# Moving the conditioning matmuls of groups 3 to 11 out of layer 0's feed-forward

## The chip, the cores and the metric

The kernel runs on one core of a Trainium2 chip. The time is that of one execution on the device, in microseconds (us); of the kernel before, three executions took 1819.61, 1820.89 and 1824.89 us, with a median of 1820.89 us.

## What is computed

Two transformer blocks of two layers each run one after the other on 256 latent tokens and 256 context tokens of width 1024. Layers 0 and 1 are the first block, layers 2 and 3 the second. The reference, cut to what matters here (`rms` is the RMS norm, `c` the conditioning vector):

```
shift1, scale1, gate1, shift2, scale2, gate2 = split(silu(c) @ w_ada[i] + b_ada[i], 6)
h = rms(x, g1) * (1 + scale1) + shift1             # norm n1
x = x + gate1 * (mixer(h) @ w_out[i])              # attention and others; layer 3: pooling
h = rms(x, g2) * (1 + scale2) + shift2             # norm n2
x = x + gate2 * (conv_ffn(h) @ w_down[i])          # w_up, 3-tap convolution, silu(gate) * value
# layers 2 and 3: the mixer's and the feed-forward's outputs pass a further RMS norm (p1, p2) before the gate
```

The six modulation vectors of a layer come from a matrix of 1024 x 6144 applied to two conditioning vectors (latent and context). They depend on no token: any time before their first use will do.

## The kernel before, in words

Activations lie transposed, with the 1024 channels as 8 tiles of 128 partitions and the tokens along the free axis: 512 tokens in layer 0, 256 from layer 1's mixer output on. Every weight block (128 output columns, 512 KB; 320 or 384 KB in w_down) is loaded by SyncE into one of four buffers `RAW`, split by ScalarE into a high part `WHI` (hi_split) and by VectorE into a remainder `WLO` (lo_split), and used by TensorE in `products`, which issues three matmuls for each of the block's k tiles: high x high, high x low and low x high. A block of w_up is 24 matmuls. A layer has the stages norm n1, projection (`proj`), attention, `w_out` (8 blocks), in layers 2 and 3 norm p1, then norm n2, `w_up` (44 blocks), `w_down` (32 blocks), and in layers 2 and 3 norm p2. Each engine has its own instruction queue, written out by hand in program order, and runs it in order; semaphores join them.

The conditioning matrices are cut into 12 groups of 8 units, three groups to a layer (3l, 3l + 1, 3l + 2). Group 0 is done at the start. A unit is 1 MB of weights, loaded by a DMA that GpSimd (POOL) issues, and four matmuls with 512 columns of weights moving (`mod_kt`, L1446; the trace shows each as two, so 8 per unit), all of a group adding up in PSUM bank 4. When 8 units are done, ScalarE copies the bank to `ROW` (`row_out`), TensorE transposes it (`mod_turn`, L1463), and VectorE adds the result to `MOD` (`mod_apply`). `derive` makes the norm's factors from `MOD`.

Before the change, groups 1 and 2 stand in layer 0's projection and use two buffers in turn, `GWA` and `GWB`. Group 3 stands in layer 0's w_out, one unit behind each block, and groups 4 to 8 and half of 9 in layer 0's w_up, one unit behind each of the 44 blocks; all these use the one buffer `GWA`, so that POOL issues the next load only when TensorE has used the unit before (L478, waiting for `gw_used`). The rest of 9, and 10 and 11, stand in layer 0's w_down with four buffers `GWH`. From layer 1 on TensorE runs no conditioning work.

A norm goes like this: squares (ScalarE), their sums by TensorE (`acc_sum`, L1470, where VectorE has added the squares up along the way; or `norm_sums`, L1478, 32 matmuls with one column), the root on ScalarE (L603), the reciprocal on VectorE (L950), its spread over the partitions by TensorE (L1493), and then VectorE (L1009, L999) and ScalarE (L616) write the 8 tiles of the next stage's input one by one.

## Time and profile before

| | us |
|---|---|
| three executions, median | 1820.89 |
| the profiled execution | 1823.76 |
| its span, first to last instruction | 1822.1 |
| TensorE busy (92% of the span) | 1671.3 |
| VectorE busy | 995.3 |
| ScalarE busy | 808.1 |
| POOL busy | 112.9 |

The profile is of one execution. "PE" is TensorE's matmuls and "PEld" its weight loads; an engine's idle time is put down to what ended it. TensorE's granted clock is 1.00 (2.4 GHz) or 0.50 (1.2 GHz) in each stretch; over the span its mean is 0.956. Its slices over the span (40 equal ones, tenths) and those of the DMA rate are

```profile
PEclk9999999899999999998999999989989999679999
GB/s 377 208 187 171 1 1 139 128 219 214 234 211 233 206 257 250 276 105 104 127 24 47 149 180 172 174 144 113 24 93 151 184 159 181 75 94 183 184 160 118
```

### The profile page before, as it was taken

What the parts mean: (1) busy time and instruction counts of PE and PEld (TensorE: products, weight loads), DVE (VectorE), ACT (ScalarE), POOL (GpSimd) and SP (SyncE); (2) the same over time, 40 slices, a digit from 0 to 9 for tenths busy, and PEclk for the clock granted to TensorE, in tenths of its full rate; (3) what the DMA queues carried; (4) which work ended last, traced back from release to release, by engine and by line L of the source; (5) the groups of instructions that cost most, each with busy time, mean ns of one, the idle gap of its engine ahead of it and who ended that gap; (6) DMA issues with size and microseconds to landing.
All of it is one profiled execution on the core that took longest, in us unless ns stands there. A gap on an engine that the chain in (4) does not pass through costs nothing.

```text
span 1822.1 us, 30331 instructions
## 1 busy us (share of the span) xinstructions
PE 1671.3 (92%) x10760; PEld 1395.0 (77%) x10760; DVE 995.3 (55%) x1746; ACT 808.1 (44%) x1406; POOL 112.9 (6%) x150
## 2 busy tenths in 40 slices
PE   3999998789999999998999999989889999589997
PEld 1786686566666666677958899979679999479997
DVE  3434863544444442226475888565556664666654
ACT  3314662333333322124364666443545555445543
POOL 0240000000000010001300000002000000000000
PEclk9999999899999999998999999989989999679999
DMA  9654003366666577733401455643035656236654
GB/s 377 208 187 171 1 1 139 128 219 214 234 211 233 206 257 250 276 105 104 127 24 47 149 180 172 174 144 113 24 93 151 184 159 181 75 94 183 184 160 118
DMA packets 72369, 285.06 MB, mean 156 GB/s; under 512 B 8001, under 2 KB 11329, under 8 KB 60513
## 3 DMA queue, kind: packets, MB, share of 16 engines
q1 hardware_dynamic: 58528, 187.31, 32.7%
q0 software_dynamic: 13760, 96.67, 15.2%
q8 instruction: 52, 0.85, 0.2%
q14 instruction: 29, 0.23, 0.0%
HBM read 282.90 MB, written 1.05 MB: 156 GB/s over the span
## 4 chain that ended last, share of the span: by engine, by line
PE 72%; DMA 14%; DVE 8%; issue 3%; ACT 2%; POOL 1%; SPq 0%; POOLq 0%; DVEq 0%; ACTq 0%
PE B L1425 17%; PE B L1427 17%; PE B L1426 17%; DMA GWA<-in_wmod 12%; PE B L1446 5%; PE B L1586 3%; PE B L1616 3%; DVE NORM L1009 2%; PE B L1604 1%; PE B L1478 1%; DMA MW<-in_wmod 1%; DVE HL L999 1%; PE B L1438 1%; PE B L1440 1%; PE B L1439 1%
## 5 line engine op out<-in xcount | busy, mean ns | idle before, releaser
L1425 PE MATMUL B<-HH,WHI 128*128 128x256 f32 (+1 forms) x1872 | 614.4, 328 | 46.6 <-DVE HL L999 24.8
L1426 PE MATMUL B<-HL,WHI 128*128 128x256 f32 (+1 forms) x1872 | 597.0, 319 | 0.0
L1427 PE MATMUL B<-HH,WLO 128*128 128x256 f32 (+1 forms) x1872 | 596.9, 319 | 0.0
L919 DVE TENSOR_TENSOR WLO<-RAW,WHI 128x1024 fp32r<-128x1024 f32 (+1 forms) x376 | 414.7, 1107 | 249.0 <-ACT WHI L559 248.1
L559 ACT ACTIVATE WHI<-RAW 128x1024 fp32r<-128x1024 f32 (+1 forms) x376 | 358.9, 959 | 256.6 <-PE B L1427 254.5
L1425 PEld LDWEIGHTS B<-HH,WHI 128*128 128x128 f32 x1872 | 363.8, 194 | 128.7 <-issue 84.3
L1427 PEld LDWEIGHTS B<-HH,WLO 128*128 128x128 f32 x1872 | 364.4, 195 | 23.3
L1426 PEld LDWEIGHTS B<-HL,WHI 128*128 128x128 f32 x1872 | 365.4, 195 | 19.0
L1425 PE MATMUL B<-MIDH,WHI 128*128 128x256 f32 (+1 forms) x704 | 220.5, 313 | 0.0
L1427 PE MATMUL B<-MIDH,WLO 128*128 128x256 f32 (+1 forms) x704 | 218.1, 310 | 0.0
L1426 PE MATMUL B<-MIDL,WHI 128*128 128x256 f32 (+1 forms) x704 | 218.0, 310 | 0.0
L1266 DVE SCALAR_TENSOR_TENSOR Y<-B,VEC,Y 128x255 f32<-128x255 f32 (+1 forms) x132 | 75.4, 571 | 220.1 <-ACT Y L805 114.7
L1425 PEld LDWEIGHTS B<-MIDH,WHI 128*128 128x128 f32 x704 | 134.4, 191 | 23.7 <-issue 17.6
L1427 PEld LDWEIGHTS B<-MIDH,WLO 128*128 128x128 f32 x704 | 134.4, 191 | 7.3
L1426 PEld LDWEIGHTS B<-MIDL,WHI 128*128 128x128 f32 x704 | 134.5, 191 | 6.2
L805 ACT ACTIVATE Y<-B,VEC 128x256 f32<-128x256 f32 (+1 forms) x88 | 54.3, 617 | 136.0 <-PE B L1427 133.6
L1586 PE MATMUL B<-KP,QK 128*128 128x512 f32 (+1 forms) x192 | 89.6, 564 | 8.7 <-ACT PB L719 7.6
L1069 DVE TENSOR_REDUCE SM<-B 128x1 f32<-128x512 f32 (+1 forms) x112 | 68.4, 611 | 42.6 <-PE B L1586 21.2
L1269 DVE SCALAR_TENSOR_TENSOR Y<-B,VEC,Y 128x255 f32<-128x255 f32 (+1 forms) x132 | 75.5, 572 | 17.9 <-DVE Y L1266 2.1
L1446 PE MATMUL B<-GWA,CV 128*32 128x512 f32 x480 | 63.9, 604 | 20.9 <-DMA GWA<-in_wmod 20.4
L719 ACT ACTIVATE PB<-B,SM 128x512 f32<-128x512 f32 (+1 forms) x112 | 69.7, 625 | 25.9 <-DVE SM L1075 15.2
L732 ACT ACTIVATE PTS<-B 128x512 f32<-128x512 f32 (+1 forms) x88 | 47.3, 538 | 54.4 <-PE B L1604 53.8
(172 smaller groups left out, 1652.7 us busy)
## 6 DMA issues: line engine op xcount, KB each, us to landing
RAW<-in_wup SPq DMA_DIRECT2D x176, 512.0 KB, 3.8
GWA<-in_wmod POOLq DMA_DIRECT2D x60, 1024.0 KB, 5.3
RAW<-in_wdn SPq DMA_DIRECT2D x64, 384.0 KB, 3.2
RAW<-in_wproj SPq DMA_DIRECT2D x44, 512.0 KB, 3.9
RAW<-in_wdn SPq DMA_DIRECT2D x64, 320.0 KB, 3.3
GWH<-in_wmod POOLq DMA_DIRECT2D x20, 1024.0 KB, 6.0
RAW<-in_wout SPq DMA_DIRECT2D x24, 512.0 KB, 3.6
MW<-in_wmod SPq DMA_DIRECT2D x4, 2048.0 KB, 18.5
```

The lines of the kernel that those rows point to most:

```text
L559: act_f(WH[s][:, 0:kts, :], RAW[s][:, 0:kts, :], ACT.Copy).then_inc(hi_done, 1)
L719: act_f(PB[:, u % 4, 0:nk], SBANK[u % 3][:, 0:nk], ACT.Exp, bias=SM[:, 320 + u:321 + u], scale=SCALE[it["kind"]], accum_out=SM[:, 384 + u: ...
L919: v.tensor_tensor(WL[s][:, 0:kts, :], RAW[s][:, 0:kts, :], WH[s][:, 0:kts, :].bitcast(F32), ALU.subtract).then_inc(lo_done, 1)
L1069: link(v.tensor_reduce(SM[:, 256 + u:257 + u], SBANK[u % 3][:, 0:nk], AX.X, ALU.max))
L1266: v.scalar_tensor_tensor(out=y[:, :, 1:256], in0=b[:, :, 0:255], scalar=w(0, which), in1=y[:, :, 1:256], op0=ALU.mult, op1=ALU.add).then_i ...
L1269: v.scalar_tensor_tensor(out=y[:, :, 0:255], in0=b[:, :, 1:256], scalar=w(2, which), in1=y[:, :, 0:255], op0=ALU.mult, op1=ALU.add).then_i ...
L1425: mm(bank[:, 0:t], wh, a, start=first and k == 0, stop=False)
L1426: mm(bank[:, 0:t], wh, b, start=False, stop=False)
L1427: ins = mm(bank[:, 0:t], wl, a, start=False, stop=stop and k == kts - 1)
L1446: ins = mm(GB[32 * j:32 * j + 32, :], CV[:, 4 * kt:4 * kt + 32], W[:, j, :], start=kt == 0, stop=kt == 7)
L1586: ins = mm(bank[:, 0:b - a], store[:, q, P * qt:P * qt + P], keys[:, k, a:b], start=True, stop=not window)
L1616: ins = mm(OBANK[it["grp"] % 2][:, c:c + it["dv"]], PTS[:, i % 2, P * k:P * k + P], it["val"](it["keys"][0] // P + k), start=k == 0, stop= ...
```

## The change

The 72 units of groups 3 to 11 are placed anew. In TensorE's order they now stand at these places:

- layer 0: two units inside w_out; two between w_out's last block and the sums of norm n2; one between the sums and the spread of n2, three behind the spread (group 3). None in w_up or w_down before the last block.
- behind the last block of w_down in layers 0, 1 and 2: two units each, then one before and two (in layer 2: five) behind the spread of the norm that follows (groups 4, 7, 10).
- layer 1: 11 units in the projection's slots 2 to 12 (rest of group 4, and group 5), 8 units behind the last 8 blocks of w_up (group 6).
- layer 2: 3 units in the projection (rest of 7), two behind w_out, one before and five behind the spread of p1 (group 8), 8 behind the last 8 blocks of w_up (group 9).
- layer 3: four units behind the spread of n1 and four behind that of p1 (group 11).

The transposes (`mod_turn`) of groups 3, 6 and 9 stand in the first block of the next w_down, those of 4, 5 and 7 in the projections, those of 8, 10 and 11 between the sums of the norms n2 of layer 2, n1 of layer 3 and n2 of layer 3. There the copy to `ROW` stands on ScalarE between the third and the fourth pair of squares, and `mod_apply` and `derive` on VectorE ahead of the reciprocal.

Each unit has a home buffer (`HOMES`): `A` and `B` as before, `H0` to `H3` in the input tiles `HH` and `HL`, `R0` to `R10` and `K0`, `K1` in the space of the attention's and feed-forward's intermediates. POOL waits before a load for the last unit with the same home, and, where the space is that of something else, for the block after which it is free. So seven loads are now issued one behind the other once w_out's first block is done in layer 0, five at the start of w_down in layer 0, four at w_out in layer 1, seven at the start of w_down in layer 1, five in w_out and eight or nine at the start of w_down in layer 2. ScalarE waits in two norms (`H_UNITS`) until the units in `H0` to `H3` are used. The total of units, matmuls and bytes is unchanged. `mod_apply` waits for its own add in the new code.

```diff
+HOMES = {1: "A B A B A B A B", 2: "A B A B A B A B", 3: "A R0 R1 R2 R3 R4 R5 R6", 4: "H0 H1 H2 H3 A B A B",
+         5: "A B A B A B A B", 6: "A R6 R8 R9 R10 A R6 R8", 7: "H0 H1 H2 H3 R6 A R8 A",
+         8: "A K0 K1 R5 R6 R8 R9 R10", 9: "A R6 R8 R9 R10 A R6 R8", 10: "H0 H1 H2 H3 R6 A R8 R9",
+         11: "R10 R6 A R8 R9 R10 R6 A"}
...
+PROJ_UNITS = [{i: (1 + i // 8, i % 8) for i in range(16)},
+              {i + 2: ((4, 5 + i) if i < 3 else (5, i - 3)) for i in range(11)},
+              {2: (7, 5), 4: (7, 6), 7: (7, 7)}]
...
-        GWB = sb("GWB", [P, 4, 512], at=w0 + 69632)
-        GWH = [sb(f"GWH{s}", [P, 4, 512], at=hhat + 8192 * s) for s in range(4)]
+        GW = {"A": GWA, "B": sb("GWB", [P, 4, 512], at=w0 + 69632)}
+        for s in range(4):
+            GW[f"H{s}"] = sb(f"GWH{s}", [P, 4, 512], at=hhat + 8192 * s)
+        for s in (0, 1, 2, 3, 4, 5, 6, 8, 9, 10):
+            GW[f"R{s}"] = sb(f"GWR{s}", [P, 4, 512], at=w0 + 8192 * s)
+        for s in range(2):
+            GW[f"K{s}"] = sb(f"GWK{s}", [P, 4, 512], at=w0 + 20480 + 8192 * s)
...
+        H_UNITS = {(1, "n1"): 28, (2, "n1"): 52}
+        TURNED = {(2, "n2"): 8, (3, "n1"): 10, (3, "n2"): 11}
...
-            def unit(u, used, W, ready):
+            def unit(g, kt):
+                u = 8 * (g - 1) + kt
+                if unit_before(u) is not None:
+                    gp.wait_ge(gw_used, unit_before(u) + 1)
+                gp.dma_start(GW[HOME[u]][:].rearrange("p a b -> p (a b)"), A["wmod1"][u * P:u * P + P, :]
+                             ).then_inc(gw_ready[HOME[u]], 16)
...
-                    if l == 0 and i < 14:
-                        unit(i + 2, i + 1, GWB if i % 2 else GWA, gwb_ready if i % 2 else gwa_ready)
+                    if l == 2 and i == 3:
+                        unit(7, 7)
+                    if l < 2 and i + 2 in PROJ_UNITS[l] and (l == 0 or i >= 1):
+                        unit(*PROJ_UNITS[l][i + 2])
...
-            with gp.Fori(16, 68, 1) as u:
-                unit(u, u, GWA, gwa_ready)
+            unit(3, 0)
+            gp.wait_ge(blk_used, OUT0[0] + 1)
+            for kt in range(1, 8):
+                unit(3, kt)
             gp.wait_ge(blk_used, DOWN0[0])
-            for s in range(4):
-                unit(68 + s, 0, GWH[s], gwh_ready[s])
-            with gp.Fori(1, 5, 1) as i:
-                for s in range(4):
-                    unit(68 + 4 * i + s, 65 + 4 * i + s, GWH[s], gwh_ready[s])
-            for l in (1, 2):
-                tables(l)
-                proj(l)
+            for kt in range(5):
+                unit(4, kt)
+            tables(1)
+            unit(4, 5)
+            proj(1)
+            gp.wait_ge(nl_ready, 8 * ROUND[1, "n1"] + 8)
+            gp.dma_start(X[:, :, 256:512], A["ctx2"].rearrange("p (k t) -> p k t", k=KT)).then_inc(ctx2_in, 16)
+            unit(6, 0)
+            gp.wait_ge(blk_used, OUT0[1] + 1)
+            for kt in range(1, 8):
+                unit(6, kt)
+            gp.wait_ge(blk_used, DOWN0[1])
+            for kt in range(7):
+                unit(7, kt)
+            tables(2)
+            proj(2)
+            for kt in range(3):
+                unit(8, kt)
+            gp.wait_ge(blk_used, OUT0[2] + 1)
+            for kt in range(3, 8):
+                unit(8, kt)
+            for kt in range(8):
+                unit(9, kt)
+            gp.wait_ge(blk_used, DOWN0[2])
+            for kt in range(8):
+                unit(10, kt)
+            unit(11, 0)
             tables(3)
+            for kt in range(1, 8):
+                unit(11, kt)
...
+                if key in H_UNITS:
+                    act.wait_ge(gw_used, H_UNITS[key])
...
+                        if c == 2 and key in TURNED:
+                            row_out(TURNED[key])
...
+                if key in TURNED:
+                    mod_apply(TURNED[key], 1)
+                    for slot in {(2, "n2"): (1, 3), (3, "n1"): (2,), (3, "n2"): (1, 3)}[key]:
+                        derive(l, slot)
...
+                        if kt == 6 and key in TURNED:
+                            mod_turn(TURNED[key])
                         norm_sum(r, kt, kt // 2 % 2, 256, kt == 0, 256 * (kt % 2))
+                if key in FILL_ROOT:
+                    fill(*FILL_ROOT[key])
                 pe.wait_ge(rr_ready, r + 1)
                 for q in range(nt):
                     ins = nc.tensor.transpose(RB[:, P * q:P * q + P], RR[:, q:q + 1].broadcast_to((P, P)), ident)
                 ins.then_inc(rb_ready, 1)
+                if key in FILL_SPREAD:
+                    fill(*FILL_SPREAD[key])
+            FILL_ROOT = {(0, "n2"): (3, [4]), (1, "n1"): (4, [2]), (2, "n1"): (7, [2]), (2, "p1"): (8, [2]),
+                         (2, "p2"): (10, [2])}
+            FILL_SPREAD = {(0, "n2"): (3, [5, 6, 7]), (1, "n1"): (4, [3, 4]), (2, "n1"): (7, [3, 4]),
+                           (2, "p1"): (8, [3, 4, 5, 6, 7]), (2, "p2"): (10, [3, 4, 5, 6, 7]),
+                           (3, "n1"): (11, [0, 1, 2, 3]), (3, "p1"): (11, [4, 5, 6, 7])}
...
-                    if l == 0:
-                        mod_unit(3, m, GWA, gwa_ready, 128 + 16 * (m + 1))
+                    if l == 0 and m in (2, 5):
+                        fill(3, [m // 3])
+                if l != 1:
+                    fill(3 if l == 0 else 8, [2, 3] if l == 0 else [0, 1])
                 acc_sum(r, t)
...
-                        if l == 0:
-                            kt = kt0 + s
-                            if kt == 0:
-                                mod_turn(group - 1)
-                            mod_unit(group, kt, GWA, gwa_ready, 128 * group - 256 + 16 * (kt + 1))
+                        if kt0 is not None:
+                            mod_unit(6 if l == 1 else 9, kt0 + s)
...
+                    with pe.Fori(0, FT // 2 - 2, 1) as i:
+                        body(i, False)
+                    body(FT // 2 - 2, False, kt0=0)
+                    body(FT // 2 - 1, True, kt0=4)
...
-                            if l == 0:
-                                b = 4 * a + s
...
+                            if l < 3 and isinstance(i, int) and i == 0 and a == 0 and s == 2:
+                                mod_turn((3, 6, 9)[l])
...
+                if l < 3:
+                    fill((4, 7, 10)[l], [0, 1])
                 acc_sum(r, tn)
```

In TensorE's queue, these rows stand in layer 0's w_up loop before: the last matmuls of a block, the transposes of the group before, the unit, and the next block.

```order
L1426 MATMUL B<-HL,WHI 128x512
L1427 MATMUL B<-HH,WLO 128x512
L1459 REGISTER_ALU
L1461 REGISTER_ALU
L1463 MATMUL B<-CST,ROW 128x128 x4
L1452 ISA
L1446 MATMUL B<-GWA,CV 32x512 x4
L1683 REGISTER_ALU
L1684 REGISTER_ALU
L1425 MATMUL B<-HH,WHI 128x512
```

And these now, where one block of that loop ends and the next begins:

```order
L1467 MATMUL B<-HL,WHI 128x512
L1468 MATMUL B<-HH,WLO 128x512
L1746 REGISTER_ALU
L1747 REGISTER_ALU
L1466 MATMUL B<-HH,WHI 128x512
```

The unit and the transposes have left; block follows block.

In TensorE's queue, between the last block of layer 2's w_out and the first of its w_up, that is around the norms p1 and n2, before:

```order
L1427 MATMUL B<-HH,WLO 128x256
L1470 MATMUL B<-CST,ACC 128x1 x2
L1493 MATMUL B<-CST,RR 128x128 x2
L1478 MATMUL B<-CST,SQ 128x1 x16
L1493 MATMUL B<-CST,RR 128x128 x2
```

and now:

```order
L1487 MATMUL B<-GWA,CV 32x512 x4
L1487 MATMUL B<-GWK_96,CV 32x512 x4
L1518 MATMUL B<-CST,ACC 128x1 x2
L1487 MATMUL B<-GWK_97,CV 32x512 x4
L1545 MATMUL B<-CST,RR 128x128 x2
L1487 MATMUL B<-GWR_91,CV 32x512 x4
L1487 MATMUL B<-GWR_92,CV 32x512 x4
L1487 MATMUL B<-GWR_93,CV 32x512 x4
L1487 MATMUL B<-GWR_94,CV 32x512 x4
L1487 MATMUL B<-GWR_95,CV 32x512 x4
L1526 MATMUL B<-CST,SQ 128x1 x12
L1511 MATMUL B<-CST,ROW 128x128 x4
```

All eight units of group 8 now stand ahead of the second norm's sums, and its transposes inside them.

In POOL's queue, in layer 1's projection, before (`RE<-SM` is one projection's roots copied out for the spread, `KP<-QK` the padded keys):

```order
L508 COPY RE<-SM 128x256
L518 TENSOR_SCALAR KP<-QK,CST 128x512 x2
L508 COPY RE<-SM 128x256
L518 TENSOR_SCALAR KP<-QK,CST 128x512 x4
L508 COPY RE<-SM 128x256
```

and now, where each load waits until TensorE has used the unit two slots back:

```order
L510 DMA GWB<-in_wmod 128x2048
L537 COPY RE<-SM 128x256
L547 TENSOR_SCALAR KP<-QK,CST 128x512 x2
L510 DMA GWA<-in_wmod 128x2048
L537 COPY RE<-SM 128x256
L547 TENSOR_SCALAR KP<-QK,CST 128x512 x4
L510 DMA GWB<-in_wmod 128x2048
```

A load stands ahead of each slot's copies, and behind the key copies of the slot before.

## Rows read from the trace of the kernel before

**Rows 1.** The page's chain that ended last, shares of the span by engine and line.
```profile
PE B L1425 17%; PE B L1427 17%; PE B L1426 17%; DMA GWA<-in_wmod 12%; PE B L1446 5%; PE B L1586 3%; PE B L1616 3%; DVE NORM L1009 2%; PE B L1604 1%; PE B L1478 1%; DMA MW<-in_wmod 1%; DVE HL L999 1%; PE B L1438 1%; PE B L1440 1%; PE B L1439 1%
```

**Rows 2.** The chain in order of time, a load in layer 0's w_up: start, duration.
```profile
409.61 5.44 DMA GWA<-in_wmod
```

**Rows 3.** TensorE's waits: layer 0's w_out, then 344.3 to 671.3: total, times, longest.
```profile
PE B L1446 <- DMA GWA<-in_wmod: 5.0, 7, 1.4
...
PE B L1446 <- DMA GWA<-in_wmod: 15.4, 33, 3.2
```

**Rows 4.** Timeline of TensorE, w_up and w_down of layer 0: start, duration.
```profile
416.67 0.39 PE L1427 MATMUL B<-HH,WLO 128*128 128x512 f32 x1
...
421.67 0.60 PE L1463 MATMUL B<-CST,ROW 128*128 128x128 f32 x4
422.19 1.07 PE L1446 MATMUL B<-GWA,CV 128*32 128x512 f32 x8
...
684.28 0.39 PE L1427 MATMUL B<-MIDH,WLO 128*128 128x512 f32 x1
684.60 1.06 PE L1446 MATMUL B<-GWH,CV 128*32 128x512 f32 x8
685.59 0.50 PE L1425 MATMUL B<-MIDH,WHI 128*128 128x512 f32 x1
685.93 0.39 PE L1426 MATMUL B<-MIDL,WHI 128*128 128x512 f32 x1
```

**Rows 5.** Windows: us, PE, PEld, DVE, ACT, POOL busy (x), PEclk, DMA share, GB/s.
```profile
350.50:671.30 320.80, 303.85 (x1432) 206.51 (x1432) 152.02 (x204) 112.10 (x151) 23.64 (x45) 0.99 0.60 211
...
1143.00:1157.00 14.00, 14.00 (x119) 14.00 (x118) 7.93 (x12) 6.65 (x10) 0.00 (x0) 1.00 0.64 183
1364.90:1494.00 129.10, 129.09 (x1056) 128.81 (x1057) 89.74 (x141) 74.42 (x116) 0.00 (x0) 0.98 0.55 163
```

**Rows 6.** Timeline of TensorE around the norms of layers 0 and 1.
```profile
344.38 1.05 PE L1470 MATMUL B<-CST,ACC 128*128 128x1 f32 x8 [1.12 <-DVE ACC L1228]
...
350.53 0.76 PE L1425 MATMUL B<-HH,WHI 128*128 128x512 f32 x1 [3.42 <-DVE HL L999]
...
358.31 0.50 PE L1425 MATMUL B<-HH,WHI 128*128 128x512 f32 x1 [0.61 <-DVE HL L999]
...
819.87 1.87 PE L1470 MATMUL B<-CST,ACC 128*128 128x1 f32 x8 [2.44 <-DVE ACC L1228]
```

**Rows 7.** Timeline of TensorE, norms p1 and n2 of layer 2, p1 and n2 of layer 3.
```profile
1350.55 0.60 PE L1470 MATMUL B<-CST,ACC 128*128 128x1 f32 x4 [0.93 <-DVE ACC L1228]
1351.71 0.43 PE L1493 MATMUL B<-CST,RR 128*128 128x128 f32 x2 [0.55 <-DVE RR L950]
1354.84 6.99 PE L1478 MATMUL B<-CST,SQ 128*128 128x1 f32 x32 [2.70 <-ACT SQ L594]
...
1599.00 4.93 PE L1478 MATMUL B<-CST,SQ 128*128 128x1 f32 x32 [1.73 <-ACT SQ L594]
...
1608.25 6.99 PE L1478 MATMUL B<-CST,SQ 128*128 128x1 f32 x32 [3.07 <-ACT SQ L594]
```

**Rows 8.** The chain at the kernel's start: 16 matmuls, two units back to back.
```profile
33.23 1.97 PE B L1446 x16
```

**Rows 9.** Windows in the stretches behind norms, columns as in rows 5.
```profile
345.50:355.50 10.00, 6.09 (x14) 3.55 (x15) 8.53 (x23) 5.46 (x13) 0.00 (x0) 0.50 0.26 100
1352.50:1369.00 16.50, 11.76 (x50) 11.02 (x51) 13.07 (x26) 7.60 (x15) 0.00 (x0) 0.50 0.21 65
```

**Rows 10.** DMA queues, 678:685, w_down of layer 0: packets, MB, share (q0 POOL's, q1 SyncE's).
```profile
q0 software_dynamic: 315, 2.31, 78.4%
q1 hardware_dynamic: 268, 0.68, 24.5%
```

**Rows 11.** Timeline of POOL, layer 1's projection, and TensorE's one wait for it.
```profile
873.40 6.74 POOL L518 TENSOR_SCALAR KP<-QK,CST 128x512 f32<-128x512 f32 x4
...
880.54 0.44 PE L1521 MATMUL B<-CST,RE 128*128 128x128 f32 x2 [1.67 <-POOL RE L508]
```

More of the change, by code:

```diff
@@ L786, in w_out, with body @@
                         tile_squares(l, "out", m, m % 2, bank)
-                    if l == 0 and m == 7:
-                        row_out(3)
             def w_up(l):
                 t = TT[l]
-                def body(i, last, group=None):
+                def body(i, last):
                     for j in range(2):
@@ L823, in body @@
                             mid_hi, 1)
-                    if group is not None:
-                        row_out(group)
                 def split(n4, s, last):
@@ L862, in body @@
                                 tile_squares(l, "down", 2 * i + a, a, banks[a])
-                            if l == 0 and a == 1 and s == 3 and not last:
-                                row_out(9 + i)
+                            if l in (1, 2) and isinstance(i, int) and i == 0 and a == 0 and s == 0:
+                                row_out(6 if l == 1 else 9)
                 loop(act, KT // 2, body, peel=True)
@@ L898, in _ @@
                 norm((l, "n2"))
+                if l == 0:
+                    row_out(3)
                 w_up(l)
@@ L1195, in attention @@
                         v_squares()
[L1196 to L1200 removed]
+                    if j == 6:
+                        if l < 2:
+                            mod_apply((2, 5)[l], 0)
+                        derive(l, 1 if l < 2 else 2)
                     if IS_L[l] and j == TT[l] // 32 + 5:
@@ L1247, in seg, with body @@
                     return ap.rearrange("p (s t) -> p s t", s=ns)
-                def body(i, last, group=None, second=0):
+                def body(i, last):
                     for j in range(2):
@@ L1292, in body @@
                                             ALU.subtract).then_inc(mid_lo, 1)
-                        if group is not None and j == 0:
-                            mod_apply(group, second)
-                if l:
-                    loop(dve, FT // 2, body)
-                else:
-                    for second, (a, b) in enumerate(((0, 3), (3, 5))):
-                        with dve.Fori(a, b, 1) as d:
-                            body(2 * d, False, group=3 + d, second=second)
-                            body(2 * d + 1, False)
-                    body(FT // 2 - 1, True, group=8, second=1)
+                loop(dve, FT // 2, body)
             def w_down(l):
@@ L1390, in _ @@
                 if l:
-                    for slot in range(2 if IS_L[l] else 4):
-                        derive(l, slot)
+                    derive(l, 0)
                 norm((l, "n1"))
```

95 lines of the change are left out of this document (37 added, 58 removed).

## The prediction

> **What bounds the kernel now.** I read the page's chain of waits first: its three largest entries are the products, 17% each, and the fourth is a DMA, the load into `GWA`, with 12% [rows 1]. Next the chain in order of time, to see what that load does in layer 0's w_up: when a unit ends, its successor's load takes 5.44 us [rows 2], and then the next unit runs 1.1 us [rows 4]. So there a block lasts as long as the single buffer's cycle. TensorE isn't idle in it, since its 24 matmuls lie beside the load; it waits only 5.0 us in w_out and 15.4 us up to the end of w_up [rows 3]. The chain's 12% is therefore no measure of the gain: nearly all of it is also matmul time. Then the timeline, for the price of the products and of a unit [rows 4], and the windows, for the stages and for who else is busy [rows 5]. TensorE sets the pace in every w_up and w_down; VectorE is busy 152 of 321 us in layer 0's w_up and 90 of 129 in layer 2's [rows 5].
>
> **Prices.** In w_up of layer 0 the start of one matmul lies 0.227 us behind the other (5.00 us for 22, to the transposes), so a block of 24 is 5.45 us [rows 4]. A unit between two blocks: from the last matmul of one to the second of the next pass 1.65 us [rows 4]; two intervals of 0.227 would pass anyway, so a unit costs 1.19 us. Two units in a row take 1.97 us [rows 8]. The transposes take 0.52 us [rows 4].
>
> **What leaves layer 0.** In w_out six of eight units go. Eight at 1.19 and 5.0 us of waits are 14.5; two come back, 2.4, and the wait for the summed squares, 1.12 us when the last unit covered part of it, becomes the 2.44 us that it is where none stands before it [rows 6], 1.3 more. Left: 10.8 us. In w_up all units go. The 44 blocks need 44 x 5.45 = 239.8 us, and the first one 4.7 more, since it goes tile by tile behind VectorE: it begins at 350.53, its sixth tile at 358.31, and with the last nine matmuls it ends near 360.7 [rows 6]. That is 244.5 against 320.8 [rows 5], so 76.3 us less. In w_down, from 671.3, where w_up ends, to the sums at 819.87 are 148.6 us [rows 5, 6]; 528 matmuls at 0.227, one set of transposes and the 2.44 us wait make 122.9. That is 25.7 less. Sum for layer 0: 112.8 us. It needs no other engine to be faster: at 245 us VectorE's 152 us are 62%, below what it carries in layer 2's w_up (70%) where TensorE doesn't wait [rows 5].
>
> **What comes to the later layers.** Thirty units stand among matmuls that set the pace: 11 and 3 in projections, 8 and 8 at the ends of two w_ups. At 1.19 us they cost 35.7 us. Four sets of transposes (groups 4, 6, 7, 9) add 2.1; those of group 5 stand before attention, where TensorE waits anyway, and I take them as nothing (0.5 if not). The `row_out` copies, `mod_apply` and `derive` go to ScalarE and VectorE while they have slack, and in the three turned norms they lie beside the sums; at nothing, 0.6 us in each if the cover is too short.
>
> Forty units stand at norms. Layer 0's n2 and the n1 of layers 1 and 2: two units behind the last block fill the 2.4 us wait. One before the spread stands in a gap of about 0.55 us [rows 7], so the spread comes 0.4 late in layers 0 and 1; those behind it fit into 3.42 us [rows 6]. ScalarE's new wait ends one unit behind the spread, when VectorE's first tile is just written. In layer 1 the sums take 1.87 us at the low clock against 1.05 in layer 0 [rows 6]; with no idle time before them I expect 1.05. Together 0.4 + 0.4 - 0.8 = 0.0 us.
>
> The p1 of layer 2 is tighter. Two units (1.97) against a wait of 0.93: 1.0 late. One against 0.55: 0.4 late. Five behind the spread, 4.9 us, against 2.70: 2.2 late. Transposes inside the sums: 0.5. Against this the 32 one-column matmuls last 6.99 us at clock 0.50, and 4.93 where they began at full clock [rows 7, 9]; I take 4.93, a gain of 2.1. Sum +2.0 us. The p2 of layer 2 with layer 3's n1 has the same pattern, +2.0. Layer 3's p1 with n2: four units, 3.9, against 3.07, transposes 0.5, the same gain of 2.1: -0.7 [rows 7]. Norms in all: +3.3 us. From both sides: if those sums all ran at full clock (about 3.5 us each), 4 us less; if the units and sums there ran at the low clock, some 17 us more, because a unit then takes about 1.8 times as long, by the ratio of the sums' 1.87 to 1.05 [rows 6].
>
> **The loads.** Before, at most four units were in flight while weights were wanted slowly. Where both queues were full, POOL's got 2.31 MB in 7 us, 330 GB/s, and the weights' 0.68 MB, 97 GB/s [rows 10]. A w_down of 256 tokens wants 183 GB/s [rows 5]. Layer 1's w_down now begins with seven loads: 7.3 MB at 330 GB/s, 22 us, in which the weights miss 86 GB/s x 22 = 1.9 MB. Four `RAW` buffers of about 0.36 MB are ahead, 1.4 MB; the 0.5 MB left take 2.6 us at 183 GB/s. Layer 2's begins with nine: 28.6 us, 2.5 MB missed, 1.0 MB not covered, 5.6 us. Bounds: nothing, if more is ahead than four buffers (four more are already split), and twice as much, if the clock falls in the waits. I take 8.2 us. The bursts in w_out (four and five loads) miss less than the four full blocks ahead; nothing. In layer 0's w_out the weights are wanted at half the rate; nothing.
>
> In layer 1's projection POOL is the narrow place: one slot's copies of the keys take 6.74 us, and TensorE once waited 1.67 us for it [rows 11]. The new loads stand between those copies, each for a unit two slots later. Two loads go out right behind such a copy, and I count 1.5 us of waits above the one that was there; between 2 less (slots longer by a unit let POOL catch up) and 8 more.
>
> **Sum.** -112.8 + 35.7 + 2.1 + 3.3 + 8.2 + 1.5 = -62.0 us. The profiled execution took 1823.76 us, so its like takes 1761.8. It is 2.9 above the median of the three; from the median 1820.89 the forecast is 1759 us.
>
> **A rule weighed.** Behind layer 0's n2 the granted clock is 0.50 for 10 us, but TensorE is busy 6.09 of them and still waits for VectorE's tiles once the clock is back [rows 6, 9]. So I give nothing for a clock that stays high there. The Trainium skill ("TensorE: Matmul & The Clock Gate", Terms) puts the penalty of throttled time at that time multiplied by one minus the granted ratio, which would be 5 us here.
>
> **Rivals.**
>
> First, more than that. The weights keep up in both w_downs (8.2 back), POOL catches up (2), the sums run at full clock (4): 14 less, 1745 us. For it: eight blocks, not four, are prepared ahead at full tilt. Against: the weights get only 97 of 183 GB/s for over 20 us. Chance 0.23.
>
> Second, the clock pays. The units keep TensorE busy behind three norms (layer 0's n2, n1 of layers 1 and 2), the clock stays at 1.00, and half of three stretches of 10 us comes back: 15 less, 1744 us. Against: VectorE's pace there, 1.57 us for a tile where three matmuls at the low clock need 1.4. Chance 0.05. This is what the skill's rule for throttled time would give.
>
> Third, the norms at the low clock and the squeeze doubled: 17 + 8 more, 1784 us. For it: sums of one column went along with a clock of 0.50 in 1352.5 to 1369 [rows 9], so that the units behind them may find it low. Against: the units are dense work just ahead. Chance 0.13.
>
> Fourth, the change doesn't do what it says in layer 0: w_up keeps a slower pace though the units are gone, because the conversion chain (ScalarE, then VectorE, for each block) was hidden by the 7 us cycle. At 6.2 instead of 5.45 us for 44 blocks, 33 more, 1792 us. Against: layer 2's w_up has a chain of the same length with blocks of 2.94 us (129.1 / 44), and TensorE is busy all the time [rows 5]. Chance 0.03.
>
> Fifth, slower than before: the late units miss their loads. Each of the 30 then waits in TensorE's queue with all later matmuls behind it. At the longest wait seen, 3.2 us [rows 3], that is 96 us: 1759 - 1.5 + 96 = 1853. It turns the sign from 2.1 us of wait for each unit (62 / 30). Against: two buffers in turn, and at the w_ups' ends five of eight units loaded long before. Chance 0.02. The skill ("DMA: Bandwidth & Descriptors", SWDGE vs HWDGE vs iDMA) says that VectorE can lock GpSimd out of the memory in which it writes its descriptors, which would delay just these loads; no row here shows it.
>
> **Chances and range.** The forecast has 0.54, with 1750 to 1768 as its own range; the rivals have 0.23, 0.05, 0.13, 0.03 and 0.02. For a range that holds 8 in 10 I go down to 1744 and up to 1778. About 0.3% is what a measurement of this kernel can tell from no change: faster 0.97, same 0.01, slower 0.02.
>
> **What would show it.** Right: no `GWA` wait in layer 0's w_up, and that stage 244 to 246 us; w_down of layer 0 about 122 us; units beside the norms at 1.0 us each and the sums of layer 2's n2 near 5 us; w_down of layer 1 and of layer 2 about 3 and 6 us longer than their 528 matmuls take at the pace of that layer's w_up (2.94 us for 24, so 64.6 us), with TensorE waiting for `WLO` and POOL's queue full beside it. Wrong: TensorE waiting for `WLO` or `drained` banks in layer 0's w_up; units of layer 1's projection waiting over 2 us each; half-clock stretches behind layer 2's p1 longer than the 16.5 us there were [rows 9]; a w_down of layer 1 with no wait at all.

## The result and the profile after

The changed kernel takes 1757.84 us (median of four executions, 1755.87 to 1759.65), the kernel before, measured beside it, 1820.25 (1817.82 to 1824.89): a ratio of 0.9654, with a 95% interval of 0.9632 to 0.9676. The forecast was 1759. The profiled execution of after took 1755.87 us with a span of 1753.7, that of before 1823.76 and 1822.1.

The page of the changed kernel: spans by engine, the clock's slices, and the two rows of the chain that answer to [rows 1]; `products` now stands in L1466 to L1468, a unit in L1487.

```profile
PE 1643.3 (94%) x10760; PEld 1389.6 (79%) x10760; DVE 995.4 (57%) x1746; ACT 808.1 (46%) x1406; POOL 112.6 (6%) x150
...
PEclk8999999999999999999989999999999999889999
...
PE 84%; DVE 9%; DMA 4%; ACT 2%; issue 1%; POOL 0%; SPq 0%; DVEq 0%; ACTq 0%
PE B L1466 22%; PE B L1468 21%; PE B L1467 21%; PE B L1487 4%; PE B L1646 3%; PE B L1676 3%; DMA RAW<-in_wdn 2%; DVE NORM L1064 2%; PE B L1664 2%; DMA MW<-in_wmod 1%; DVE SM L1124 1%; PE B L1479 1%; PE B L1481 1%; PE B L1480 1%; DVE HL L1054 1%
```

The load into `GWA` is gone from the chain, and the products went from 17% to 21 or 22% each. What is new in it is the DMA `RAW<-in_wdn`, 2%: SyncE's weights for w_down.

Windows of after (us, PE, PEld, DVE, ACT, POOL busy, PEclk, DMA share, GB/s): layer 0's w_up, the 10 us around its start, then the w_downs of layers 1 and 2.

```profile
341.08:585.18 244.10, 241.10 (x1056) 197.74 (x1057) 151.05 (x197) 109.09 (x145) 0.00 (x0) 1.00 0.31 91
...
336.00:346.00 10.00, 7.52 (x47) 2.98 (x48) 8.47 (x23) 5.49 (x13) 0.00 (x0) 1.00 0.01 2
...
1050.00:1120.00 70.00, 67.04 (x556) 64.51 (x548) 37.09 (x51) 32.07 (x44) 4.06 (x8) 1.00 0.82 280
1419.00:1492.00 73.00, 68.99 (x557) 66.06 (x549) 29.94 (x41) 31.02 (x51) 5.04 (x10) 0.98 0.82 286
```

Layer 0's w_up takes 244.10 us where it took 320.80 [rows 5], with the same VectorE work (151 us); VectorE's share rose from 47% to 62%.

The stages, each from the start of one marking instruction to that of the next (a stage's first product, or the first sum of a norm), in the traces of before and after:

| stage | before | after | difference | forecast |
|---|---|---|---|---|
| w_out, layer 0 | 62.6 | 50.6 | -12.0 | -10.8 |
| w_up, layer 0 | 320.8 | 244.1 | -76.7 | -76.3 |
| w_down, layer 0 | 148.6 | 122.7 | -25.8 | -25.7 |
| all norms, from their first sum on, with layer 3's pooling | 97.4 | 93.2 | -4.2 | +1.3 |
| layer 1, projection to w_out | 182.1 | 194.4 | +12.3 | +15.1 |
| w_up, layers 1 and 2 | 258.6 | 276.8 | +18.2 | +19.0 |
| w_down, layers 1 and 2 | 130.1 | 142.4 | +12.4 | +10.2 |
| layer 2, projection to w_out | 136.5 | 141.0 | +4.5 | +5.1 |
| all before layer 0's w_out, all of layer 3 behind its n2 | 485.5 | 488.4 | +2.9 | 0 |
| sum | 1822.1 | 1753.7 | -68.4 | -62.0 |

(The forecast's transposes and late sums are counted here in the stage in which they stand.) The spans differ by 6 us more than forecast, the medians by 62.4 as forecast: the profiled execution of before lay 3.5 us above its median, that of after 2.0 below.

TensorE's timeline around layer 0's n2, start and duration, which answers to [rows 6]:

```profile
332.55 1.92 PE L1487 MATMUL B<-GWR,CV 128*32 128x512 f32 x16
335.04 1.05 PE L1518 MATMUL B<-CST,ACC 128*128 128x1 f32 x8 [0.56 <-DVE ACC L1282]
336.02 1.06 PE L1487 MATMUL B<-GWR,CV 128*32 128x512 f32 x8
337.02 0.65 PE L1545 MATMUL B<-CST,RR 128*128 128x128 f32 x4
337.60 2.78 PE L1487 MATMUL B<-GWR,CV 128*32 128x512 f32 x24
341.08 0.47 PE L1466 MATMUL B<-HH,WHI 128*128 128x512 f32 x1 [0.70 <-DVE HL L1054]
...
345.72 0.50 PE L1466 MATMUL B<-HH,WHI 128*128 128x512 f32 x1 [0.61 <-DVE HL L1054]
...
348.88 0.50 PE L1466 MATMUL B<-HH,WHI 128*128 128x512 f32 x1 [0.61 <-DVE HL L1054]
```

Six units fill the waits: the one for the summed squares, 1.12 us before behind one unit and 2.44 where no unit stood before it [rows 6], is 0.56, and 3.42 became 0.70. In the kernel before, the clock was 0.50 from 5 us ahead of w_up's first product to 5 us behind it [rows 9]; the same stretch of after, 336 to 346 above, has 1.00. And yet the tiles begin at the same pace: the sixth 7.80 us behind the first (341.08, 348.88), before 7.78 (350.53, 358.31 [rows 6]). In that kernel's trace the second and the fourth tile, 3.15 us apart at half clock, were

```profile
352.01 0.79 PE L1425 MATMUL B<-HH,WHI 128*128 128x512 f32 x1
...
355.16 0.67 PE L1425 MATMUL B<-HH,WHI 128*128 128x512 f32 x1
```

and in the changed kernel's two intervals at full clock are 3.16 us (345.72 to 348.88). TensorE waits about 0.6 us for VectorE's `HL` before each of these tiles now: VectorE sets the pace. What gained from the clock is the spread, which waits for no tile: 0.65 us above, and 1.11 in the kernel before:

```profile
346.00 1.11 PE L1493 MATMUL B<-CST,RR 128*128 128x128 f32 x4 [0.57 <-DVE RR L950]
```

The same around layer 2's p1 and n2, which answers to [rows 7]:

```profile
1268.04 1.06 PE L1487 MATMUL B<-GWK,CV 128*32 128x512 f32 x8
1269.04 0.43 PE L1545 MATMUL B<-CST,RR 128*128 128x128 f32 x2
1269.40 4.50 PE L1487 MATMUL B<-GWR,CV 128*32 128x512 f32 x40
1273.83 2.91 PE L1526 MATMUL B<-CST,SQ 128*128 128x1 f32 x24
1276.60 0.63 PE L1511 MATMUL B<-CST,ROW 128*128 128x128 f32 x4
1277.07 0.95 PE L1526 MATMUL B<-CST,SQ 128*128 128x1 f32 x8
```

The 32 one-column matmuls took 6.99 us at half clock; they take 2.91 + 0.95 = 3.86 now. The sums begin late, because of five units, and end early all the same.

### The profile page after: what moved, and what is told of

The parts are those of the page before. It is cut to its first block, busy times and chain, and to the rows that moved or that the text cites. A ratio compares the mean times of both kernels' runs of the same rounds, so it can differ in the third digit from the quotient of the medians.

```text
span 1753.7 us, 29978 instructions
## 1 busy us (share of the span) xinstructions
PE 1643.3 (94%) x10760; PEld 1389.6 (79%) x10760; DVE 995.4 (57%) x1746; ACT 808.1 (46%) x1406; POOL 112.6 (6%) x150
## 4 chain that ended last, share of the span: by engine, by line
PE 84%; DVE 9%; DMA 4%; ACT 2%; issue 1%; POOL 0%; SPq 0%; DVEq 0%; ACTq 0%
PE B L1466 22%; PE B L1468 21%; PE B L1467 21%; PE B L1487 4%; PE B L1646 3%; PE B L1676 3%; DMA RAW<-in_wdn 2%; DVE NORM L1064 2%; PE B L1664 2%; DMA MW<-in_wmod 1%; DVE SM L1124 1%; PE B L1479 1%; PE B L1481 1%; PE B L1480 1%; DVE HL L1054 1%
## 5 line engine op out<-in xcount | busy, mean ns | idle before, releaser
L1466 PE MATMUL B<-HH,WHI 128*128 128x256 f32 (+1 forms) x1872 | 607.4, 324 | 36.4 <-DVE HL L1054 21.2
L1468 PE MATMUL B<-HH,WLO 128*128 128x256 f32 (+1 forms) x1872 | 594.2, 317 | 0.0
L1466 PEld LDWEIGHTS B<-HH,WHI 128*128 128x128 f32 x1872 | 362.5, 194 | 94.3 <-issue 45.8
L1468 PEld LDWEIGHTS B<-HH,WLO 128*128 128x128 f32 x1872 | 363.1, 194 | 22.2
L1466 PE MATMUL B<-MIDH,WHI 128*128 128x256 f32 (+1 forms) x704 | 220.0, 313 | 7.0 <-DVE WLO L969 6.9
L1468 PE MATMUL B<-MIDH,WLO 128*128 128x256 f32 (+1 forms) x704 | 218.5, 310 | 0.0
L1466 PEld LDWEIGHTS B<-MIDH,WHI 128*128 128x128 f32 x704 | 135.0, 192 | 17.0 <-DVE WLO L969 8.4
L1468 PEld LDWEIGHTS B<-MIDH,WLO 128*128 128x128 f32 x704 | 135.0, 192 | 6.8
L1124 DVE TENSOR_REDUCE SM<-B 128x1 f32<-128x512 f32 (+1 forms) x112 | 68.4, 611 | 41.4 <-PE B L1651 20.8
L878 ACT ACTIVATE MIDH<-Y 128x256 f32 (+3 forms) x88 | 40.8, 463 | 57.5 <-DVE Y L1333 57.5
```

What stands on the lines that cost most here:

```text
L1124: link(v.tensor_reduce(SM[:, 256 + u:257 + u], SBANK[u % 3][:, 0:nk], AX.X, ALU.max))
L1466: mm(bank[:, 0:t], wh, a, start=first and k == 0, stop=False)
L1468: ins = mm(bank[:, 0:t], wl, a, start=False, stop=stop and k == kts - 1)
```

## The experiments

Each ran beside the kernel before on the same chip, in three sets. The median of the kernel before was 1819.1 us in the first (spaced loads, half the bytes, no unit in slot 8), 1818.93 in the second (the changed kernel once more, earlier loads, idle places, the three together) and 1819.73 in the third (short units, the second version). Ratios are to it, with their 95% intervals. In the diffs, + is the experiment and ... stands for parts left out.

**The changed kernel once more**, as the control.

> The changed kernel once more, for the comparison on this chip: 1756 to 1759, ratio to the kernel before 0.965.

1755.62 us, ratio 0.9656 (0.9635 to 0.9677), span 1754.0. Every stage lies within 0.5 us of the first trace, but for layer 0 up to n2 (3 us shorter) and layer 1's projection to w_out (3.0 us longer; its wait for `GWB` was 3.2 us).

**Loads spaced.** The bursts of seven and nine loads in the w_downs of layers 1 and 2 become one load per four and three blocks.

```diff
-            gp.wait_ge(blk_used, DOWN0[1])
             for kt in range(7):
+                gp.wait_ge(blk_used, DOWN0[1] + 4 * kt)
                 unit(7, kt)
...
```

> The changed kernel, with the loads of groups 7, 10 and 11 at the start of layer 1's and layer 2's w_down not issued one behind the other but one for every 4 blocks (layer 1) or 3 blocks (layer 2). Theory: the waits of 3.0 and 4.0 us for WLO in these two stages, the slower blocks beside them and the low clock behind them come from POOL's loads taking the DMA engines from the weights. Then both stages lose their waits, w_down of layer 1 gets some 4 us shorter and that of layer 2 some 6 us, and the time falls from 1757.8 to about 1748. Rival: the waits come from the transposes in the first block or from the order of the conversions; then they stay, and the time with them (1757 to 1759).

1749.7 us, ratio 0.9627 (0.9609 to 0.9646). Queues in 1051 to 1063, w_down of layer 1, first of the changed kernel, then of the spaced one (packets, MB, share; q1 is SyncE's, q0 POOL's):

```profile
q0 software_dynamic: 530, 3.95, 83.9%
q1 hardware_dynamic: 292, 0.73, 15.3%
```

```profile
q1 hardware_dynamic: 576, 1.44, 39.0%
q0 software_dynamic: 222, 1.69, 37.9%
```

And TensorE's wait in that w_down, in the changed kernel (the spaced one has none for `WLO`):

```profile
PE B L1466 <- DVE WLO L969: 3.0, 3, 1.6
```

With a burst in flight the weights get 0.73 MB in these 12 us, 61 GB/s; without it 1.44 MB, and TensorE doesn't wait for them. The burst does it in two ways. SyncE issued a load at 1052.63, and no packet of it moved before 1056.0; in the spaced kernel one issued at 1052.60 had moved 148 packets by then. After that both queues are busy and share by packets, not by bytes. From 1057 to 1072 in the changed kernel:

```profile
q0 software_dynamic: 643, 4.65, 74.2%
q1 hardware_dynamic: 639, 1.60, 27.3%
```

The stage went from 69.97 to 66.09 us, that of layer 2 from 72.47 to 66.00: the squeeze cost 3.9 + 6.5 = 10.4 us. The stages repeat well: layer 1's w_down took 69.9 to 70.1 us in all six traces that have the whole burst and 66.1 in the four in which it is spaced or halved. By medians the spaced kernel is only 5.9 us below the control, and 8.1 below the first measurement; its profiled execution was its fastest, 3.8 us below its median, so the size rests on the stages. Of the 10.4 us TensorE's waits for `WLO` are 3.0 + 4.0 = 7.0. Another 1.5 is a stretch at half clock in layer 2, right behind the last of these waits, where 16 matmuls start 0.216 us apart instead of 0.120:

```profile
1449.00:1452.40 3.40, 3.40 (x19) 3.40 (x18) 0.82 (x1) 0.79 (x2) 0.00 (x0) 0.51 0.93 364
```

The remaining 1.9 weren't traced. Without the squeeze the two stages take 66 us against 65.6 and 64.5 before; 0.5 of that are the transposes.

**Half the bytes, after.** Each unit of groups 3 to 11 loads 0.5 MB and multiplies it twice.

```diff
-                gp.dma_start(GW[HOME[u]][:].rearrange("p a b -> p (a b)"), A["wmod1"][u * P:u * P + P, :]
+                gp.dma_start(GW[HOME[u]][:, 0:(2 if g > 2 else 4), :].rearrange("p a b -> p (a b)"),
+                             A["wmod1"][u * P:u * P + P, 0:(1024 if g > 2 else 2048)]
...
```

> The changed kernel, but each unit of groups 3 to 11 loads only half of its weights (0.5 MB) and its four matmuls use that half twice; matmuls and waits are as many as before. Theory: what loads cost in the changed kernel is the squeeze in the two w_downs (some 10 us) and the wait in layer 1's projection (up to 4 us): 1744 to 1748. Rival: the loads cost nothing and the waits have another reason: 1757 to 1759. A second rival: the loads also slow the matmuls or conversions elsewhere, then well below 1740.

1741.52 us, ratio 0.9583 (0.9561 to 0.9606). The w_downs take 66.09 and 65.83 us, the same as with spaced loads, by another way; layer 1's projection to w_out 191.06 instead of 194.43, with one wait of 1.4 us for `GWB`. So the bytes cost about 14 us in the changed kernel: 10.5 in the two w_downs and 3.4 there.

**Half the bytes, before.** The same in the kernel before.

> The kernel before, but each unit of groups 3 to 11 loads only half of its weights and uses that half twice. Theory: a load of half the size ends before the block's matmuls do, so the waits of 20.4 us for GWA go and nothing else: about 1820 - 21 = 1799, and w_up of layer 0 takes about 44 x 6.65 + 5 + 3 = 301 us instead of 321. Rival: the load chain (12% of the span in the chain of waits) is what sets layer 0's time, and most of the 62 us of the change come from its absence; then the time falls below 1780.

1797.11 us, ratio 0.9894 (0.9873 to 0.9915). TensorE's waits for `GWA` between 350 and 627, first of the kernel before, then with half the bytes:

```profile
PE B L1446 <- DMA GWA<-in_wmod: 13.4, 28, 3.2
```

```profile
PE B L1448 <- DMA GWA<-in_wmod: 1.4, 1, 1.4
```

The w_up of layer 0 takes 302.03 us, 18.8 less, and 58 are still to go to 244.1; 44 units at 1.19 us, 52.4, and their transposes are nearly all of them. So of the 76.7 us that left w_up the load cycle alone holds about a quarter. That is not yet its share, since with it gone TensorE's own work binds; the next experiment takes the two in the other order.

**Short units, before.** The units of groups 3 to 11 multiply only 32 of 512 columns each time; the loads stay whole.

```diff
-                    ins = mm(GB[32 * j:32 * j + 32, :], CV[:, 4 * kt:4 * kt + 32], W[:, j, :], start=kt == 0,
+                    ins = mm(GB[32 * j:32 * j + 32, 0:cols], CV[:, 4 * kt:4 * kt + 32], W[:, j, 0:cols], start=kt == 0,
...
```

> The kernel before, but the units of groups 3 to 11 multiply only 32 of the 512 columns of each part (some 0.2 us instead of 1.19); their loads and waits stay whole. Theory: in layer 0's w_up a block can't be shorter than the single buffer's cycle, load 5.4 us and issue 0.6 behind the unit, so about 6.3 us for a block instead of 7.05 and 283 us for the stage, not the 245 of the changed kernel; w_down, with four buffers, loses its 20 units whole, 18 us. In all about 60 us less than before, 1758. Rival: the load chain doesn't bind, a block falls to the matmuls' 5.45 us plus 0.3: 253 us for w_up and about 1728 in all.

1767.43 us, ratio 0.9709 (0.9685 to 0.9733). The w_up takes 287.24 us; it would take some 253 if only TensorE's work counted (244 and 44 short units at 0.2 us, an estimate). Its timeline, at one block's end and the next one's beginning:

```profile
386.69 0.39 PE L1427 MATMUL B<-HH,WLO 128*128 128x512 f32 x1
389.74 0.33 PE L1446 MATMUL B<-GWA,CV 128*32 128x32 f32 x8 [2.67 <-DMA GWA<-in_wmod]
390.01 0.80 PE L1425 MATMUL B<-HH,WHI 128*128 128x512 f32 x1
```

A block now lasts 287.24 / 44 = 6.53 us: a load of 5.2 us (the median there) and what lies between two of them. So the kernel before had both limits: with hardly any unit matmuls the single buffer's cycle binds (6.53 a block), without the cycle the matmuls do (302.03 / 44 = 6.86). Only with both gone is a block 5.55. Short units alone took 33.5 us from w_up, halved loads alone 18.8, both gone 76.7. So the cycle costs 19 us if it is taken away first; taken last it is the 43 us left, less some 11 for the short units and the transposes (at 0.2 and 0.52 us, an estimate), 32. After a wait of 2.67 us the products run at half clock (0.80 us); over this w_up the granted clock is 0.98, which is at most 6 us of the 32.

**Short units at the norms, after.** 38 of the 40 units at norms multiply 32 columns (the expectation says 36; the trace has 38).

```diff
-                    mod_unit(g, kt)
+                    mod_unit(g, kt, 512 if (g, kt) in ((3, 0), (3, 1), (4, 0), (7, 0)) else 32)
...
```

> The changed kernel, but 36 of the 40 units at the norms multiply only 32 of the 512 columns of each part; loads and waits stay whole. Theory: these units stand in idle time, so their length costs little: 1 us each where they delay sums (behind w_out of layer 2, behind w_down of layer 2), 2 us at each spread of layer 2's p1, layer 2's p2 and layer 3's p1, and against this the clock falls to 0.50 there again and the one-column sums take 5 to 7 us instead of 3.9. Net between 0 and 5 us less than the changed kernel. Rival one: units cost their length everywhere, 36 us less. Rival two: the higher clock that they bring is worth more than they cost; then the time rises by 3 us or more.

1761.11 us, ratio 0.968 (0.9658 to 0.9702): 5.5 above the control by medians, 4.4 by ratios and by spans (1758.4 and 1754.0). The two intervals overlap, and the two ran in different sets, so the size is uncertain; the stages below show that it is real. Less work, more time. Its windows behind the norms of layers 2 and 3, then those of the changed kernel:

```profile
1266.00:1286.00 20.00, 14.44 (x109) 13.08 (x110) 14.56 (x32) 9.95 (x20) 2.61 (x5) 0.57 0.89 355
1499.00:1545.00 46.00, 23.24 (x179) 21.22 (x179) 32.03 (x55) 18.01 (x35) 1.57 (x3) 0.61 0.53 204
```

```profile
1266.00:1286.00 20.00, 17.54 (x130) 11.28 (x123) 15.03 (x32) 10.54 (x20) 2.64 (x5) 0.83 0.90 351
1499.00:1545.00 46.00, 31.26 (x200) 21.04 (x199) 33.86 (x58) 19.95 (x38) 1.76 (x4) 0.78 0.57 220
```

The sums of n2 in layer 2 in the kernel with short units:

```profile
1268.22 0.76 PE L1487 MATMUL B<-GWR,CV 128*32 128x32 f32 x40
1270.99 5.28 PE L1526 MATMUL B<-CST,SQ 128*128 128x1 f32 x24 [2.01 <-ACT SQ L648]
```

Five units take 0.76 us instead of 4.50, TensorE idles 2.01, and the clock falls: 24 sums take 5.28 us instead of 2.91. The stages p1 with n2 of layer 2, p2 with n1 of layer 3, and pooling to n2 of layer 3 grow by 1.6, 1.9 and 3.0. Where TensorE would wait anyway, the units are worth more than they cost, through the clock. (The other stages, where short units save time, give 2 us back.)

**No unit in slot 8** of layer 1's projection; the later ones stand one slot on.

```diff
-              {i + 2: ((4, 5 + i) if i < 3 else (5, i - 3)) for i in range(11)},
+              {i + 2 + (i > 5): ((4, 5 + i) if i < 3 else (5, i - 3)) for i in range(11)},
...
```

> The changed kernel, with no unit in slot 8 of layer 1's projection: the units from there on stand one slot later (9 to 13). Theory: the unit of slot 8 waited 2.4 us because its load stood in POOL's queue behind the key copies, and the wait brought a stretch of low clock of 3.4 us (1.7 us). One more slot lets POOL catch up: 3 to 4 us less, about 1754. Rival: POOL is late for good, the wait moves to slot 9, and the time stays at 1757 to 1758.

1754.63 us, ratio 0.966 (0.9643 to 0.9677), and layer 1's projection to w_out takes 194.31 us, as it did (194.43): the rival came true. The wait moved with the load: first the changed kernel, then this one.

```profile
769.95 1.93 PE L1487 MATMUL B<-GWB,CV 128*32 128x512 f32 x8 [2.40 <-DMA GWB<-in_wmod]
```

```profile
772.68 1.46 PE L1487 MATMUL B<-GWB,CV 128*32 128x512 f32 x8 [2.87 <-DMA GWB<-in_wmod]
```

**Loads of slots 8 and 9 earlier**, between the second and the third key copy. POOL's timeline in the changed kernel, which answers to [rows 11]:

```profile
756.75 6.83 POOL L547 TENSOR_SCALAR KP<-QK,CST 128x512 f32<-128x512 f32 x4
763.53 0.59 POOL L510 DMA_DIRECT2D GWB<-in_wmod  x1
764.13 0.41 POOL L537 COPY RE<-SM 128x256 f32<-128x256 f32 x1
764.51 6.28 POOL L547 TENSOR_SCALAR KP<-QK,CST 128x512 f32<-128x512 f32 x4
770.74 0.59 POOL L510 DMA_DIRECT2D GWA<-in_wmod  x1
```

The load for slot 8 goes out at 763.53, behind four key copies, and the unit gets it at 769.95.

```diff
                     gp.tensor_scalar(KP[:, k, :], QK[:, q, :], m, None, ALU.mult).then_inc(keys_ready, 1)
+                    if l == 1 and q and j == 1:
+                        unit(*PROJ_UNITS[1][q + 7])
...
```

> The changed kernel, with two loads of layer 1's projection (for the units of slots 8 and 9) issued by POOL between the second and third key copy of the slot before, not behind the fourth. Theory: TensorE's wait of 2.4 us in slot 8 is the time that the load stood behind POOL's copies (its buffer was free at 758.5, POOL reached it at 763.5). Issued some 3 us earlier it lands in time, and the stretch of low clock behind the wait goes too: 3 to 4 us less than the changed kernel. Rival: POOL's total work, not its order, is late; then the wait goes to the spread of the roots (RE) and the time stays.

1751.4 us, ratio 0.9629 (0.9608 to 0.9651), 4.2 below the control by medians, 0.5 by spans (the profiled execution was its slowest). The wait in slot 8 is gone, but slot 9 waits 2.8 us, since its load goes out at 767.70 behind more copies. What it is worth stays open.

**Idle places.** Ten units go from places where TensorE is busy, or from layer 3's p1, to where it waits: three of group 6 and two of 9 to the norms n2 of layers 1 and 2, one of group 7 to the spread of layer 2's n1, four of 11 to the spread of layer 3's n1.

```diff
...
-                           (3, "n1"): (11, [0, 1, 2, 3]), (3, "p1"): (11, [4, 5, 6, 7])}
+                           (3, "n1"): (11, [0, 1, 2, 3, 4, 5, 6, 7])}
...
-                        if kt0 is not None:
+                        if kt0 is not None and kt0 + s >= (3 if l == 1 else 2):
```

> The changed kernel with ten units in other places: three of group 6 from the end of layer 1's w_up to its norm n2 (one before the sums, two behind the spread), two of group 9 from the end of layer 2's w_up to behind the spread of its n2, one of group 7 from the projection to behind the spread of n1, and four of group 11 from behind layer 3's p1 to behind its n1, where TensorE idles 8.9 us. Theory: a unit costs what it takes (1.15 us) only where matmuls stand ready; six units leave such places, 6.9 us, the four of group 11 delayed the sums by about 2 us, and the idle times hold them all but for some tenths: 8 to 9 us less than the changed kernel. Rival: the norms are full, and each unit put there delays the sums or the spread by its own length; then no change, or up to 3 us slower.

1749.42 us, ratio 0.9626 (0.9604 to 0.9647), 6.2 below the control. The w_ups of layers 1 and 2 are 3.8 and 3.9 us shorter, the norms behind layer 2's w_out 1.3 longer. Group 11 was a miss: the units at layer 3's n1 came before their loads.

```profile
1504.44 1.06 PE L1487 MATMUL B<-GWR,CV 128*32 128x512 f32 x8 [2.70 <-DMA GWR<-in_wmod]
1506.92 1.93 PE L1487 MATMUL B<-GWR,CV 128*32 128x512 f32 x8 [1.42 <-DMA GWR<-in_wmod]
```

That stage grew by 3.1 us; pooling to n2 shrank by 1.7. It could have shrunk by more: with no units ahead, the sums of layer 3's n2 ran at half clock again, 7.73 us with the transposes among them where the changed kernel has 4.19. That is the short units' effect once more, by another edit.

```profile
1532.11 5.28 PE L1526 MATMUL B<-CST,SQ 128*128 128x1 f32 x24 [3.07 <-ACT SQ L648]
```

**The three together** (spaced, early, idle places).

> The changed kernel with all three: the loads of the w_downs of layers 1 and 2 one for every 4 or 3 blocks, the two early loads in layer 1's projection, and the ten units in other places. If the three costs are separate stages' (theory), they add up: 10.4 in the w_downs, 3.5 in the projection, 8.5 at the norms, 22 us less than the changed kernel, about 1735. Rival: what is saved in one place comes back as waits in the next (loads now closer to their use); then above 1742.

1738.27 us, ratio 0.9569 (0.9543 to 0.9595), 17.4 below the control where the theory had 22. A new wait appeared in layer 1's n2 (5.07 us instead of 3.55): ScalarE waited 2.73 us for a weight block while the loads of group 6 ran.

**The second version**: spaced, slot 9 left free with slot 8's load early, idle places without group 11, and group 6's loads spread over w_out and w_up.

```diff
             for kt in range(1, 8):
+                gp.wait_ge(blk_used, OUT0[1] + 3 * kt - 2 if kt < 3 else UP0[1] + 4 * kt)
                 unit(6, kt)
...
```

> As the combined kernel before, but group 11 stays where the changed kernel has it, slot 9 of layer 1's projection has no unit (slots 2 to 8 and 10 to 13 have), and the loads of group 6 are spread too (one in w_out's first block and one three blocks on, the rest in w_up). Theory: the four units of group 11 moved into layer 3's idle stretch waited for their loads and made it 3.1 us longer against 1.7 us won behind; back in their place they give 1.5 us. The wait of slot 9 goes (2 to 3 us), and so does the late weight block of layer 1's w_out. About 20 us less than the changed kernel, 1735. Rival: the projection's wait moves on once more, and the sum stays at 1738.

1739.06 us, ratio 0.9553 (0.9535 to 0.9571): n2 of layer 1 is back at 3.43 us, and no unit of layer 1's projection waits. Its profiled execution has one thing against it: in layer 2's n2 the sums, with all units of group 8 ahead of them as in the changed kernel, took 5.92 us with the transposes instead of 4.19, and p1 with n2 took 17.05 us against 15.00 for the same order in idle places. The clock fell there in this trace and in none of the eight others that have whole units ahead of these sums; why stays open. The two versions can't be told apart by their times; either is some 17 us below the changed kernel.

## Why the prediction was right

The mechanism was the one named, and the large terms, those of layer 0 and of the two w_ups, were right within about 1 us each. That the total came within 1.2 us is in part luck: the norms were 5.5 us better than forecast and layer 1's projection 2.8, the two w_downs 2.2 worse, and the traces' stages sum to 6.4 us more than forecast, of which 5.5 is how the two profiled executions lie to their medians.

- **What leaves layer 0.** Forecast -112.8, measured -114.5. The w_up goes at TensorE's pace as worked out (244.5; 244.10). Of the reading of the chain, "its 12% is no measure of the gain": half the bytes brought 22 us (1819.1 to 1797.11); 12% of the span would be 219. The other half of the reading, that a block lasted as long as the single buffer's cycle, holds too: with short units the cycle still kept w_up at 287 us.
- **Units among matmuls.** 1.19 us each was forecast. Eight in a w_up cost 9.1 us, 1.13 each. In layer 1's projection the trace shows +12.3 for a forecast of 15.1, but before varies there: two experiments on the kernel before that leave layer 1 as it is took 179.7 and 180.0 us for it, where the profiled execution took 182.1. Against those it is +14.5 (17 to 18 in the control).
- **The norms.** The one mechanism read wrongly. The forecast took 4.93 us for the sums of layers 2 and 3, as if they began at full clock and lost it; they took 3.85 or 3.86 in all three (without the transposes among them), with the units in front: 3.2 us better in all. The spreads of layer 0's n2 and of the n1 of layers 1 and 2 took 0.65 us instead of 1.11, 1.4 more. These are the largest parts of the 5.5 us by which all norms are better than forecast. The bound "all sums at full clock, 4 us less" was the right end, and the short units showed that it is the units that hold the clock: without their columns the three stages lose 6.4 us. Not all of it held: at layer 3's p1 the four units found the clock low and took 5.7 us, not the 3.9 forecast.

```profile
1536.98 4.85 PE L1487 MATMUL B<-GWR,CV 128*32 128x512 f32 x24
1541.67 1.03 PE L1487 MATMUL B<-GWA,CV 128*32 128x512 f32 x8
```

- **The squeeze.** Forecast 8.2, measured 10.4 by spacing the loads, 10.5 by halving them. The weights' rate was right: 107 GB/s with both queues busy (1.60 MB in 15 us), for 97 forecast [rows 10]. The bursts were longer, 26.2 and 32.9 us from first issue to last landing instead of 22 and 28.6, and in each the weights' queue moved nothing for over 3 us at the start; over the bursts (26 and 33 us) they got 2.90 and 3.76 MB. The forecast's own sum with these figures, an estimate, gives 2.5 + 4.8 = 7.3 us, and the waits for `WLO` are 7.0. The term was too small by what it put at nothing beside the waits, 3.4 us of slower matmuls; 1.5 of them are the stretch at half clock, which its upper bound had named.
- **The projection's wait.** Forecast 1.5 above before; the trace has one of 2.4 us and the 1.7 of before gone, the control one of 3.2. Its place, a load behind four key copies, was as argued. What removing it brings was not settled.
- **What remains.** Before layer 0's w_out the two traces differ by 2.7 us; but for `mod_apply`'s wait no work is changed there, and the control's trace up to n2 is 3 us shorter than that of after.

The rivals: "more than that" was right in the norms and wrong in the w_downs, which waited. "The clock pays" fell, and for the reason given against it: the clock did stay at 1.00 behind layer 0's n2, and the tiles came at the same pace. By the Trainium skill's rule ("TensorE: Matmul & The Clock Gate", Terms) 10 us at half clock cost 5; here w_up took only 0.4 us less than a forecast that counted nothing for the clock. At the one-column sums, where nothing else sets the pace, the trace comes near the rule: 6.99 us became 3.86. By it they would be 3.5 us, an estimate. "Norms at the low clock" had the sign of the effect wrong in layer 2, and was right about the units of layer 3's p1, 1.8 us. "Held by conversions" fell with 244.10 us. Of "late units" the projection had one case; the idle places at layer 3's n1 made some more, with waits up to 2.7 us.

## What to carry to other kernels

When a DMA heads the chain but the engine beside it is 95% busy, halve its bytes in thought and ask what stands behind: here halving the loads alone gave a quarter of w_up's gain, shortening the filler's matmuls alone less than half, and only both together the whole. Two limits that lie close can't be given shares. Put filler work where the engine would wait, and give its loads a pace of their own, since a burst on one queue slows the other for as long as it lasts. Count a filler at a wait as a gain if matmuls that no other engine paces follow it: here it kept the clock up for the sums behind it in all traces but one.

## What was not expected of the hardware

- Low clock isn't time lost by itself: two tiles took 3.16 us at 1.00 and 3.15 at 0.50, where VectorE feeds.
- Two DMA queues that are both busy shared packets evenly here, not bytes: 643 packets to 639 in 15 us, and so 4.65 MB (310 GB/s) for POOL's, with packets of 7.2 KB, and 1.60 MB (107 GB/s) for SyncE's, with packets of 2.5 KB.
- A load issued into a burst of the other queue waited 3.4 us for its first packet to move, beside the sharing.
- Less TensorE work (38 short units) made the kernel 4 to 5 us slower.
